# Weight sums of a one-level block product, two of four made by adding DMAs: a hybrid decoder layer on one Trainium2 core

## Chip, cores and metric

One NeuronCore of a Trainium2 chip runs the whole program in a single launch. The metric is the device time of that launch in microseconds. The program before has a median of 1208.45 us over three runs (1207.03 to 1209.76).

## What is computed

One decoder layer over 592 tokens (16 meta tokens, 8 x 8 sample tokens, 512 prompt tokens), model width 1024, all in float32:

```python
h += 0.5 * SwiGLU_1(RMSNorm(h))          # w1, w3: 1024 x 2816, w2: 2816 x 1024
h += mixer(RMSNorm(h))                   # gated DeltaNet heads and a causal convolution
h += 0.5 * SwiGLU_2(RMSNorm(h))
y  = RMSNorm(h)

def swiglu_half(h, g, w1, w3, w2):
    u = rmsnorm(h, g)
    return h + 0.5 * ((jax.nn.silu(u @ w1) * (u @ w3)) @ w2)
```

The change touches the two SwiGLU stages alone (called stages 0 and 1 in the code; of stage 1 the 16 meta tokens are dropped, so it works on 576 columns).

## The kernel before

**Number format.** Each float32 product is three float32r products: a value is split into hi (a cast on ScalarE) and lo (the rest, a subtraction on VectorE), and TensorE adds hi*hi, hi*lo and lo*hi.

**Tiles and parts.** The 2816 hidden features are 22 feature tiles of 128. A tile has two weight units in DRAM, of 128 x 1024 values (512 KB) each: unit u holds the tile's columns of w1, unit u+1 those of w3. The tiles go in parts of 4, 4, 3, 3, 4 and 4 (`PARTS`); behind each part its share of the product with w2 is made for all 8 output tiles (`down`) and added to `h` (`down_add`, L1968). The four tiles of the first part are multiplied directly.

**Seven products.** The 18 tiles of the other five parts are multiplied by a one-level scheme with seven block products in place of eight. The pair of units is taken as a 2 x 2 block matrix: A11 and A12 are the upper and lower half of the w1 unit (rows 0:4 and 4:8 of `KT`), A21 and A22 those of the w3 unit. The tokens are cut in two halves. The scheme needs four sums of weight blocks, S3, S1, S2 and S4, and four of activation blocks, T1 to T4, which are made once per stage (`half_sum`). Each block product, a seventh, is 12 matmuls of 128 x 296 (`seventh`, L839). TensorE's order within a tile is S3, S2 (behind it the mark "m6"), A12, S1 ("m5"), A11 of the next tile ("m1") or a first piece of `down`, S4 ("c1"), A22 ("c2"); see `by_sevenths` and `seventh_order`. The marks are values of the semaphore `seventh_done`.

**Where the weights lie.** `raw` and `raw2` take the two units of a tile as they come from DRAM, by turns. A set of seven pieces of 128 x 512 holds the blocks in hi and lo: `s_hi` and `s_lo`, each twice, by turns as well (`piece`, the number of the turn is `use`). The float32 sums (`s_sum`) lie in the same bytes as `s_lo`, which overwrites them.

**Who makes the sums.** VectorE makes all four, 128 x 512 each, from raw:

```python
V.tensor_tensor(s_f32(t, S3), r[:, 0, 0:4], r[:, 1, 0:4], ALU.subtract)      # sums_first, L1984
V.tensor_tensor(s_f32(t, S1), r[:, 1, 0:4], r[:, 1, 4:8], ALU.add)           # sums_first, L1985
V.tensor_tensor(s_f32(t, S2), s_f32(t, S1), raw_tile(t.u)[:, 0, 0:4], ALU.subtract)   # sum_two, L1989
V.tensor_tensor(s_f32(t, S4), raw_tile(t.u)[:, 0, 4:8], s_f32(t, S2), ALU.subtract)   # sum_four, L1993
```

While TensorE works on a tile, VectorE and ScalarE prepare the next one (`nxt` in `by_sevenths`). On ScalarE the order is: cast of A11/A12 (`hi_first`, L1393), cast of g, two copies out of PSUM behind m6 (L1478, L1480), cast of S3/S1 (`hi_sums(nxt, 0)`, L1398), copy behind m5 (L1485), cast of S2/S4 (`hi_sums(nxt, 1)`, L1398), `seed` (L1472), cast of A22 (L1402), SiLU (L1432). On VectorE: `c21` (L2018) and the gate product (L1928) of the tile before, the first two sums, rest of A11/A12 (L1997), rest of g (L1937), S2 (L1989), rest of S3/S1 (L2005), S4 (L1993), `c22` (L2024), rest of S2/S4 (L2005), rest of A22 (L2010). TensorE does not start A22 of a tile until `c22` of that tile is done. Both orders are written out by hand; each engine works its own queue strictly in order.

**Loads.** SyncE issues all weight loads in one order (`load_used`, L654): both units of a tile, once the last rest of the tile two turns back has been taken (`w_lo_ready`). GpSimd does nothing in these stages; its first work is the sum of squares behind stage 0.

## Time and profile before

| | |
|---|---|
| median of 3 runs | 1208.45 us (1207.03 to 1209.76) |
| the profiled execution | 1213.22 us, its span 1211.1 us |
| TensorE busy | 1194.6 us, 99% of the span, 8832 matmuls |
| VectorE busy | 787.3 us, 65%, 1155 instructions |
| ScalarE busy | 515.8 us, 43% |
| GpSimd busy | 75.2 us, 6% |
| DMA | 99.68 MB, mean 82 GB/s |
| mean granted TensorE clock | 0.991 |

The span runs from the first to the last instruction of one profiled execution. Busy times of the engines overlap. Matmuls are pipelined, so the duration of one is longer than the distance from one to the next.

### The profile page before, as it was taken

How to read it: one execution, taken by the hardware profiler on the slowest of the kernel's cores; microseconds unless marked ns; L12 is line 12 of the kernel's file. 1: busy time of each engine (PE TensorE's matmuls, PEld its weight loads, DVE VectorE, ACT ScalarE, POOL GpSimd, SP SyncE). 2: the span in 40 equal slices, each digit the busy share in tenths (PEclk: the TensorE clock that was granted, in tenths of full speed). 3: DMA queues.
4: the chain of work that ended last, by engine and by line, in shares of the span. 5: the costliest groups of instructions: out<-in, count | busy, mean ns of one | idle time of the engine just before them, and what ended most of it. 6: DMA issues, size and time to landing. Idle time of an engine off the chain costs nothing.

```text
span 1211.1 us, 21067 instructions
## 1 busy us (share of the span) xinstructions
PE 1194.6 (99%) x8832; PEld 1167.1 (96%) x8832; DVE 787.3 (65%) x1155; ACT 515.8 (43%) x820; POOL 75.2 (6%) x58
## 2 busy tenths in 40 slices
PE   9999999999999999999999998999999999999997
PEld 9999999999999998999989897999999999999997
DVE  6897565767566644666447786537785667675764
ACT  6345343535344542333443444433444344353355
POOL 0000000000000300000125210220000000000003
PEclk9999999999999999999999999999999999999999
DMA  5322212222223422111600002322123131222112
GB/s 189 127 86 73 105 61 96 88 105 79 96 79 109 127 73 79 60 53 54 125 4 1 1 2 88 117 84 88 53 105 109 72 116 62 96 104 105 70 71 78
DMA packets 39212, 99.68 MB, mean 82 GB/s; under 512 B 12112, under 2 KB 15568, under 8 KB 39120
## 3 DMA queue, kind: packets, MB, share of 16 engines
q1 hardware_dynamic: 38064, 96.00, 23.5%
q10 hardware_dynamic: 1056, 2.36, 0.5%
q8 instruction: 70, 1.15, 0.4%
q14 instruction: 22, 0.18, 0.1%
HBM read 92.91 MB, written 5.44 MB: 81 GB/s over the span
## 4 chain that ended last, share of the span: by engine, by line
PE 96%; DVE 2%; ACT 1%; issue 1%; DMA 0%; POOLq 0%; DVEq 0%; POOL 0%; SPq 0%
PE ps L839 34%; PE ps L806 21%; PE ps L755 20%; PE ps L951 12%; PE ps L1329 4%; PE ps L719 1%; PE ps L1135 1%; PE ps L1343 1%; PE ps L1241 1%; ACT x_hi L1411 1%; DVE w_lo L1906 1%; DVE h L1968 1%; PE ps L921 0%; PE ps L973 0%; DMA h<-x_t 0%
## 5 line engine op out<-in xcount | busy, mean ns | idle before, releaser
L839 PE MATMUL ps<-x_hi,s_hi 128*128 128x296 f32 (+1 forms) x576 | 171.2, 297 | 0.2
L839 PE MATMUL ps<-x_hi,s_lo 128*128 128x296 f32 (+1 forms) x576 | 170.9, 297 | 0.0
L839 PE MATMUL ps<-x_lo,s_hi 128*128 128x296 f32 (+1 forms) x576 | 170.9, 297 | 0.0
L755 PE MATMUL ps<-x_hi,w_hi 128*128 128x296 f32 (+1 forms) x608 | 136.8, 306 | 0.3 <-DVE x_lo L1911 0.3
L755 PE MATMUL ps<-x_lo,w_hi 128*128 128x296 f32 (+1 forms) x608 | 133.0, 300 | 0.0
L755 PE MATMUL ps<-x_hi,w_lo 128*128 128x296 f32 (+1 forms) x608 | 132.5, 299 | 0.0
L839 PE MATMUL ps<-t_hi,s_hi 128*128 128x296 f32 (+1 forms) x432 | 128.3, 297 | 0.0
L839 PE MATMUL ps<-t_hi,s_lo 128*128 128x296 f32 (+1 forms) x432 | 128.1, 297 | 0.0
L839 PE MATMUL ps<-t_lo,s_hi 128*128 128x296 f32 (+1 forms) x432 | 128.0, 296 | 0.0
L2005 DVE TENSOR_TENSOR s_lo<-s_sum,s_hi 128x1024 fp32r<-128x1024 f32 x72 | 88.2, 1225 | 44.2 <-ACT s_hi L1398 41.5
L839 PEld LDWEIGHTS ps<-x_hi,s_hi 128*128 128x128 f32 x576 | 108.4, 188 | 0.6 <-issue 0.6
L839 PEld LDWEIGHTS ps<-x_hi,s_lo 128*128 128x128 f32 x576 | 108.4, 188 | 0.0
L839 PEld LDWEIGHTS ps<-x_lo,s_hi 128*128 128x128 f32 x576 | 108.3, 188 | 0.0
L755 PEld LDWEIGHTS ps<-x_hi,w_hi 128*128 128x128 f32 x608 | 99.8, 191 | 3.7 <-issue 2.8
L1378 ACT CAST w_hi<-raw 128x1024 fp32r<-128x1024 f32 x52 | 54.1, 1043 | 114.3 <-PE ps L755 83.0
L755 PEld LDWEIGHTS ps<-x_lo,w_hi 128*128 128x128 f32 x608 | 99.9, 191 | 0.0
L755 PEld LDWEIGHTS ps<-x_hi,w_lo 128*128 128x128 f32 x608 | 99.2, 190 | 0.0
L1398 ACT CAST s_hi<-s_sum 128x1024 fp32r<-128x1024 f32 x72 | 76.0, 1056 | 46.0 <-DVE s_sum L1993 42.3
L1968 DVE SCALAR_TENSOR_TENSOR h<-ps,h 128x592 f32<-128x592 f32 (+1 forms) x92 | 69.5, 761 | 23.4 <-PE ps L806 18.1
L806 PE MATMUL ps<-g_hi,w_hi 128*128 128x296 f32 (+1 forms) x384 | 83.1, 298 | 0.0
L806 PE MATMUL ps<-g_lo,w_hi 128*128 128x296 f32 (+1 forms) x384 | 82.9, 297 | 0.0
L806 PE MATMUL ps<-g_hi,w_lo 128*128 128x296 f32 (+1 forms) x384 | 82.6, 296 | 0.0
(316 smaller groups left out, 2558.8 us busy)
## 6 DMA issues: line engine op xcount, KB each, us to landing
raw<-weights SPq DMA_DIRECT2D x150, 512.0 KB, 3.4
raw<-weights SPq DMA_DIRECT2D x16, 384.0 KB, 3.5
S<-states SPq DMA_DIRECT2D x1, 2048.0 KB, 11.8
new_state<-S ACTq DMA_DIRECT2D x1, 2048.0 KB, 6.9
y_t<-h SPq DMA_DIRECT2D x4, 336.0 KB, 2.3
h<-x_t SPq DMA_DIRECT2D x4, 296.0 KB, 4.7
h<-x_t SPq DMA_DIRECT2D x2, 592.0 KB, 7.5
raw<-weights SPq DMA_DIRECT2D x4, 256.0 KB, 5.2
```

The source lines that it names most:

```text
L719: last = nc.tensor.matmul(ps[:, u, half, 0:HALF], w[:, u, k, :], x[:, k, half * HALF:(half + 1) * HALF], start=(k == 0 and n == 0), stop=( ...
L755: last = nc.tensor.matmul(ps[:, slot if out is None else out, half, 0:w_half], w[:, slot, k, :], x[:, k, a:a + w_half], start=(k == 0 and ...
L806: last = nc.tensor.matmul(ps[:, slot, half, 0:w_half], w[:, (k % 2) * n + i, :], x[:, i, token_half(half, lo)], start=(i == 0 and r == 0), ...
L839: last = nc.tensor.matmul(out, w[:, k, :], x[:, k, :], start=(start and k == 0 and r == 0), stop=(k == KT // 2 - 1 and r == 2), skip_group ...
L951: return nc.tensor.matmul(out, lhsT, rhs, start=start, stop=stop, skip_group_check=True)
L1135: last = nc.tensor.transpose(half_bank(a + q, 0, n)[:, hd, :], inverse(t)[:, 2 * q + hd, 0:n], m("ident", n))
L1241: nc.tensor.matmul(ps[:, OUT_SLOT[j], half, 0:w_half], w[:, j, k, :], x[:, k - 4, a:a + w_half], start=(k == 4 and r == 0), stop=False, sk ...
L1329: last = nc.tensor.matmul(ps[:, OUT_SLOT[j], half, 0:w_half], w[:, j, k, :], x[:, kk, a:a + w_half], start=(u >= 2 and k == 4 and r == 0), ...
L1378: nc.scalar.copy(w_hi[:, slot], raw[:, slot % 2]).then_inc(w_hi_ready, 1)
L1398: nc.scalar.copy(piece(0, t.use, at, 2), piece(2, t.use, at, 2)).then_inc(piece_s_hi, 1)
L1968: V.scalar_tensor_tensor(two(h[:, k, lo:]), both(slot, lo), 0.5, two(h[:, k, lo:]), ALU.mult, ALU.add).then_inc(psum_free, part.step(k))
L2005: V.tensor_tensor(piece(1, t.use, at, 2), piece(2, t.use, at, 2), piece(0, t.use, at, 2).bitcast(F32), ALU.subtract).then_inc(piece_s_lo, 1)
```

## The change

1. S3 and S1 are no longer made by VectorE. SyncE loads the upper half of the w3 unit (A21, 256 KB) into both places in `s_sum` (`load_bases`), and GpSimd issues two DMAs from DRAM that add to what lies there: A11 to the place of S3, A22 to that of S1 (`add_bases`, `accum_op=ALU.add`). The upper half of the w3 unit is no longer loaded into `raw`.
2. Since these DMAs add, the second block row (the w3 unit) is taken with the other sign: S2 and S4 become additions, T1, T2 and T4 change sign (two of the activation sums become a `scalar_tensor_tensor`), and the result is taken from `h` with -0.5 in place of +0.5.
3. The waits follow. A base load of a tile waits until the block product that used this place two turns back is done ("m6" for S3, "m5" for S1, `sum_free`), and for the base load before it. An adding DMA waits for its base load and for the adding DMA before it. ScalarE's cast of S3/S1 and VectorE's S2 wait for both adding DMAs of the tile (`base_sums`).
4. The first two units of w2 in a set move from the pieces A11, A12, S3, S1 to A11, A12, S2, S4 (`down_unit`), so that the places of S3 and S1 are free during `down`.
5. Some semaphores are merged (`tables_in`, `wba_ready`).

```diff
+def summed(what, t):
+    return 2 * t + ("S2", "S4").index(what) + 1
...
             if (part.use + part.n + v // 2 + 1) % 2:
-                return [x[1][:, KT * (v % 2):KT * (v % 2 + 1)] for x in (s_hi, s_lo)]
+                at = KT // 2 * (S2 if v % 2 else A11)
+                return [x[1][:, at:at + KT] for x in (s_hi, s_lo)]
...
+        def sum_free(eng, t, at):
+
+            back = t.use - 2
+            while back >= 0:
+                for before in FFN[t.part.stage][1:]:
+                    if before.use <= back < before.use + before.n:
+                        eng.wait_ge(seventh_done, SEVENTH["m6" if at == S3 else "m5", before.tiles[back - before.use].t])
+                        return
+                back -= 2
+            eng.wait_ge(unit_done, FFN[t.part.stage][0].count(3) if back == -1 else t.part.base)
...
+            def load_tile(t):
+
+                part, use = t.part, t.use
+                if use > 1:
+                    sp.wait_ge(w_lo_ready, t.u - 2)
+                elif use == 1:
+                    sp.wait_ge(t_vector, t_dve("lo T4", part.stage))
+                for j in range(2):
+                    if use == 0:
+                        sp.wait_ge(w_lo_ready, t.u + j - 1)
+                    to, sem_in = (raw2, raw2_in) if use % 2 else (raw, raw_in[j])
+                    rows = slice(KT // 2 if j else 0, KT)
+                    sp.dma_start(to[:, j, rows], weights[t.u + j][:, rows]).then_inc(sem_in, 16)
+
+            def load_bases(t):
+
+                for i, at in enumerate((S3, S1)):
+                    sum_free(sp, t, at)
+                    if t.t or i:
+                        sp.wait_ge(base_in, 32 * t.t + 16 * i)
+                    sp.dma_start(piece(2, t.use, at), weights[t.u + 1][:, 0:KT // 2]).then_inc(base_in, 16)
+
             def load_parts(stage):
 
                 for part in FFN[stage][1:]:
                     for t in part.tiles:
-                        load_used(part, t.u, t.use, KT)
+                        for load in (load_bases, load_tile) if t.use == 1 else (load_tile, load_bases):
+                            load(t)
...
             def hi_sums(t, which):
-                act.wait_ge(weight_sums, 3 * t.t + (3 if which else 1))
+                if which:
+                    act.wait_ge(weight_sums, summed("S4", t.t))
+                else:
+                    act.wait_ge(base_sums, 32 * (t.t + 1))
...
-                V.scalar_tensor_tensor(two(h[:, k, lo:]), both(slot, lo), 0.5, two(h[:, k, lo:]), ALU.mult,
+                V.scalar_tensor_tensor(two(h[:, k, lo:]), both(slot, lo), -0.5 if part.at else 0.5, two(h[:, k, lo:]), ALU.mult,
                                        ALU.add).then_inc(psum_free, part.step(k))
...
-            def sums_first(t):
-
-                r = raw_tile(t.u)
-                raw_ready(t.u)
-                raw_ready(t.u + 1)
-                set_free(dve, t.part, t.use)
-                V.tensor_tensor(s_f32(t, S3), r[:, 0, 0:4], r[:, 1, 0:4], ALU.subtract)
-                V.tensor_tensor(s_f32(t, S1), r[:, 1, 0:4], r[:, 1, 4:8], ALU.add).then_inc(weight_sums, 1)
...
+            def sum_two(t):
+                dve.wait_ge(base_sums, 32 * (t.t + 1))
+                V.tensor_tensor(s_f32(t, S2), s_f32(t, S1), raw_tile(t.u)[:, 0, 0:4], ALU.add).then_inc(weight_sums, 1)
+
+            def sum_four(t):
+                dve.wait_ge(weight_sums, summed("S2", t.t))
+                V.tensor_tensor(s_f32(t, S4), raw_tile(t.u)[:, 0, 4:8], s_f32(t, S2), ALU.add).then_inc(weight_sums, 1)
...
-                out, a, b = {"T3": (t_sum[3][:, :, 0:n], x22, x12), "T1": (x12, x12, x11), "T2": (x22, x22, x12),
-                             "T4": (t4_f32(lo), x21, x22)}[q]
-                V.tensor_tensor(out, a, b, ALU.subtract).then_inc(t_vector, 1)
+                out, a, b = {"T3": (t_sum[3][:, :, 0:n], x22, x12), "T1": (x12, x11, x12), "T2": (x22, x12, x22),
+                             "T4": (t4_f32(lo), x22, x21)}[q]
+                if q in ("T2", "T4"):
+                    V.scalar_tensor_tensor(out, a, -1.0, b, ALU.mult, ALU.subtract).then_inc(t_vector, 1)
+                else:
+                    V.tensor_tensor(out, a, b, ALU.subtract).then_inc(t_vector, 1)
...
+            def add_bases(stage):
+
+                for part in FFN[stage][1:]:
+                    for t in part.tiles:
+                        for i, (at, j, k) in enumerate(((S3, 0, 0), (S1, 1, KT // 2))):
+                            pool.wait_ge(base_in, 32 * t.t + 16 * (i + 1))
+                            if t.t or i:
+                                pool.wait_ge(base_sums, 32 * t.t + 16 * i)
+                            pool.dma_start(piece(2, t.use, at), weights[t.u + j][:, k:k + KT // 2],
+                                           accum_op=ALU.add).then_inc(base_sums, 16)
+
+            add_bases(0)
             sum_squares(1)
...
             sum_squares(2, LATE)
+            add_bases(1)
             sum_squares(3, LATE)
```

How the instructions stand, on VectorE, in the second part of stage 0, from the end of the preparation of its second tile to that of its third. Before:

```order
L2018 TENSOR_TENSOR work<-ps,work 128x296
L1928 TENSOR_TENSOR work<-work 128x592
L1984 TENSOR_TENSOR s_sum<-raw 128x512
L1985 TENSOR_TENSOR s_sum<-raw 128x512
L1997 TENSOR_TENSOR s_lo<-raw,s_hi 128x1024
L1937 TENSOR_TENSOR g_lo<-work,g_hi 128x592
L1989 TENSOR_TENSOR s_sum<-s_sum,raw 128x512
L2005 TENSOR_TENSOR s_lo<-s_sum,s_hi 128x1024
L1993 TENSOR_TENSOR s_sum<-raw,s_sum 128x512
L2024 TENSOR_TENSOR work<-ps,work 128x296
```

With the change, the same place:

```order
L2053 TENSOR_TENSOR work<-ps,work 128x296
L1970 TENSOR_TENSOR work<-work 128x592
L2032 TENSOR_TENSOR s_lo<-raw,s_hi 128x1024
L1979 TENSOR_TENSOR g_lo<-work,g_hi 128x592
L2022 TENSOR_TENSOR s_sum<-s_sum,raw 128x512
L2040 TENSOR_TENSOR s_lo<-s_sum,s_hi 128x1024
L2026 TENSOR_TENSOR s_sum<-raw,s_sum 128x512
L2059 TENSOR_TENSOR work<-ps,work 128x296
```

The two first sums are gone; from S2 (now L2022) to `c22` (now L2059) the same four instructions stand in the same order.

On SyncE's queue, from the first tile of that part to the loads of its w2 units, with the change (before, there stand 18 rows of L654, 128x1024, one behind the other up to the end of that part and the first tiles of the next; `s_sum` are the base loads):

```order
L684 DMA raw<-weights 128x1024
L684 DMA raw<-weights 128x512
L692 DMA s_sum<-weights 128x512 x4
L684 DMA raw<-weights 128x1024
L684 DMA raw<-weights 128x512
L684 DMA raw<-weights 128x1024
L684 DMA raw<-weights 128x512
L692 DMA s_sum<-weights 128x512 x2
L684 DMA raw<-weights 128x1024
L684 DMA raw<-weights 128x512
L692 DMA s_sum<-weights 128x512 x2
L670 DMA raw<-weights 128x1024 x4
```

Each tile has two base loads behind its own loads; only the second tile has them ahead of these. The load of a fourth tile now stands behind the base loads of the third.

## Rows read from the trace of the kernel before

**Rows 1.** The page: busy time of each engine, and the granted clock in 40 slices.

```profile
PE 1194.6 (99%) x8832; PEld 1167.1 (96%) x8832; DVE 787.3 (65%) x1155; ACT 515.8 (43%) x820; POOL 75.2 (6%) x58
...
PEclk9999999999999999999999999999999999999999
```

**Rows 2.** What TensorE waited for: us in total, times, longest (8 rows in all).

```profile
PE ps L951 <- DVE qo L2446: 2.5, 2, 2.0
PE ps L1095 <- DVE d_kg L2387: 2.2, 1, 2.2
...
PE ps L951 <- ACT d_inv L1745: 0.2, 1, 0.2
```

**Rows 3.** Busy time by stretch: PE, PEld, DVE, ACT, POOL; clock, DMA share, GB/s.

```profile
20.00:60.00 40.00, 40.00 (x296) 40.00 (x295) 32.66 (x39) 16.67 (x22) 0.00 (x0) 1.00 0.37 123
...
100.00:140.00 40.00, 40.00 (x296) 40.00 (x295) 26.58 (x35) 19.76 (x30) 0.00 (x0) 1.00 0.27 100
...
470.00:500.00 30.00, 30.00 (x176) 26.41 (x175) 16.16 (x35) 11.58 (x24) 0.00 (x0) 0.89 0.17 53
```

**Rows 4.** Groups of VectorE's instructions by line: busy us, mean ns; idle before.

```profile
L2005 DVE TENSOR_TENSOR s_lo<-s_sum,s_hi 128x1024 fp32r<-128x1024 f32 x72 | 88.2, 1225 | 44.2 <-ACT s_hi L1398 41.5
...
L1984 DVE TENSOR_TENSOR s_sum<-raw 128x512 f32<-128x512 f32 x36 | 24.7, 686 | 18.7 <-PE ps L806 17.3 <-DMA raw<-weights 1.4
L1985 DVE TENSOR_TENSOR s_sum<-raw 128x512 f32<-128x512 f32 x36 | 24.6, 684 | 0.0
```

**Rows 5.** Timeline of ScalarE, marks m6 and m5 of two tiles: start us, us.

```profile
91.48 0.39 ACT L1478 COPY ps<-ps 128x296 f32<-128x296 f32 x1 [1.94 <-PE ps L839]
...
94.74 0.41 ACT L1485 COPY work<-ps 128x296 f32<-128x296 f32 x1 [1.60 <-PE ps L839]
...
102.89 0.39 ACT L1478 COPY ps<-ps 128x296 f32<-128x296 f32 x1 [1.19 <-PE ps L839]
...
103.49 1.06 ACT L1398 CAST s_hi<-s_sum 128x1024 fp32r<-128x1024 f32 x1
```

**Rows 6.** Timeline of VectorE, third tile of the second part prepared.

```profile
100.20 0.78 DVE L1928 TENSOR_TENSOR work<-work 128x592 f32<-128x592 f32 x1
...
103.92 0.68 DVE L1989 TENSOR_TENSOR s_sum<-s_sum,raw 128x512 f32<-128x512 f32 x1
104.71 1.22 DVE L2005 TENSOR_TENSOR s_lo<-s_sum,s_hi 128x1024 fp32r<-128x1024 f32 x1
105.85 0.68 DVE L1993 TENSOR_TENSOR s_sum<-raw,s_sum 128x512 f32<-128x512 f32 x1
106.59 0.47 DVE L2024 TENSOR_TENSOR work<-ps,work 128x296 f32<-128x296 f32 x1
```

**Rows 7.** TensorE: timeline, first matmul of A22 of the second tile; first product with S3.

```profile
109.21 0.30 PE L839 MATMUL ps<-x_hi,s_hi 128*128 128x296 f32 x1
...
L839 PE MATMUL ps<-t_hi,s_hi x432: 290/297/303, 88.0 to 1172.5; 128*128 128x296 f32 x72, 128*128 128x288 f32 x72
```

**Rows 8.** The loads of L654, and DMA issues by size: KB each, median us to landing.

```profile
L654 SPq DMA_DIRECT2D raw<-weights x112: 327/333/1425, 56.8 to 1165.8; - x112
...
DMA to landing us min/median/max: 2.9/3.9/6.5
y_t<-h SPq DMA_DIRECT2D x4, 240.0 KB, 2.3
```

**Rows 9.** Starts of the stage: VectorE and SyncE's timeline, then GpSimd's first work.

```profile
61.44 1.23 DVE L1906 TENSOR_TENSOR w_lo<-raw,w_hi 128x1024 fp32r<-128x1024 f32 x1 [0.29 <-ACT w_hi L1378]
...
78.11 0.68 DVE L1989 TENSOR_TENSOR s_sum<-s_sum,raw 128x512 f32<-128x512 f32 x1
...
98.11 0.80 SPq L654 DMA_DIRECT2D raw<-weights  x2
...
394.72 0.76 POOL L2593 COPY ssum<-sq 128x592 f32<-128x592 f32 x1 [394.27 <-ACT sq L1412]
```

More of the change, by code:

```diff
@@ L514, in build @@
         psum_free = sem("psum_free")
-        x_in = [sem(f"x_in{q}") for q in range(len(X_PIECES))]; vec_in = sem("vec_in"); norm_in = sem("norm_in"); hist_in = sem("hist_in"); state_in = sem("state_in")
+        x_in = [sem(f"x_in{q}") for q in range(len(X_PIECES))]; vec_in = sem("vec_in"); norm_in = sem("norm_in"); hist_in = sem("hist_in")
         ones_set = sem("ones_set")
@@ L522, in build @@
         raw2_in = sem("raw2_in")
-        weight_sums = sem("weight_sums"); piece_s_hi = sem("piece_s_hi"); piece_s_lo = sem("piece_s_lo")
+        base_in = sem("base_in"); base_sums = sem("base_sums"); weight_sums = sem("weight_sums"); piece_s_hi = sem("piece_s_hi"); piece_s_lo = sem("piece_s_lo")
         seventh_done = sem("seventh_done"); copies_out = sem("copies_out"); halves_out = sem("halves_out")
@@ L526, in build @@
         g_hi_ready = sem("g_hi_ready"); g_ready = sem("g_ready")
-        wba_hi_ready = sem("wba_hi_ready"); wba_ready = sem("wba_ready")
+        wba_ready = sem("wba_ready")
         pads_set = sem("pads_set")
@@ L532, in build @@
         sig_ready = sem("sig_ready"); c_in_ready = sem("c_in_ready")
-        dft_in = sem("dft_in"); taps_ps = sem("taps_ps"); taps_ready = sem("taps_ready")
+        tables_in = sem("tables_in"); taps_ps = sem("taps_ps"); taps_ready = sem("taps_ready")
         win_ps = sem("win_ps"); win_ready = sem("win_ready"); spec_ps = sem("spec_ps"); spec_ready = sem("spec_ready")
@@ L681, in _ @@
             sp.wait_ge(unit_done, U_GLU)
-            sp.dma_start(dft[:], dfts).then_inc(dft_in, 16)
+            sp.dma_start(dft[:], dfts).then_inc(tables_in, 16)
             with sp.Fori(0, (U_QKV + 4 - U_GLU - 4) // 2) as i:
@@ L689, in _ @@
             sp.wait_ge(unit_done, U_GLU)
-            sp.dma_start(S[:, :, 1:NG, :], states).then_inc(state_in, 16)
+            sp.dma_start(S[:, :, 1:NG, :], states).then_inc(tables_in, 16)
             sp.wait_ge(c_in_ready, NC_)
@@ L914, in gate_products @@
             def gate_products():
-                pe.wait_ge(wba_ready, 1)
+                pe.wait_ge(wba_ready, 2)
                 pe.wait_ge(rstd_ready, 2)
@@ L955, in tap_transforms @@
             def tap_transforms():
-                pe.wait_ge(dft_in, 16)
+                pe.wait_ge(tables_in, 16)
                 pe.wait_ge(psum_free, U_QKV)
@@ L1252, in state_heads @@
                 if hd == 0:
-                    pe.wait_ge(state_in, 16)
+                    pe.wait_ge(tables_in, 32)
                     pe.wait_ge(s["ek_ready"], 1)
@@ L1574, in _ @@
             nc.scalar.activation(expa[:], v("a_log", 0, H), ACT.Exp)
-            nc.scalar.copy(wba[:, :, 0:2 * H], v("w_ba", 0, KT * 2 * H).rearrange("p (k c) -> p k c", k=KT)).then_inc(wba_hi_ready, 1)
+            nc.scalar.copy(wba[:, :, 0:2 * H], v("w_ba", 0, KT * 2 * H).rearrange("p (k c) -> p k c", k=KT)).then_inc(wba_ready, 1)
             root(0)
@@ L1976, in s_f32, with lo_first @@
                 return piece(2, t.use, at)
[L1978 to L1980 removed]
+            def sum_two(t):
[4 more added lines that the diff above has]
+                V.tensor_tensor(s_f32(t, S4), raw_tile(t.u)[:, 0, 4:8], s_f32(t, S2), ALU.add).then_inc(weight_sums, 1)
+            def lo_first(t):
                 raw_ready(t.u)
[L1982 removed]
                 set_free(dve, t.part, t.use)
[L1984 to L1995 removed]
                 dve.wait_ge(piece_s_hi, 3 * t.t + 1)
@@ L2003, in lo_sums @@
                 if not which:
-                    dve.wait_ge(weight_sums, 3 * t.t + 2)
+                    dve.wait_ge(weight_sums, summed("S2", t.t))
                 V.tensor_tensor(piece(1, t.use, at, 2), piece(2, t.use, at, 2), piece(0, t.use, at, 2).bitcast(F32),
@@ L2034, in by_sevenths @@
                 if nxt:
-                    sums_first(nxt)
                     lo_first(nxt)
@@ L2091, in down_first @@
                 half_lo("B21", stage)
-                sums_first(t)
                 down_add(part, 1)
@@ L2113, in down_mid @@
                     down_add(part, k)
-                sums_first(t)
                 down_add(part, 3)
@@ L2188, in _ @@
                 add_square(k)
-            dve.wait_ge(wba_hi_ready, 1)
+            dve.wait_ge(wba_ready, 1)
             V.tensor_tensor(wba[:, :, 2 * H:], v("w_ba", 0, KT * 2 * H).rearrange("p (k c) -> p k c", k=KT),
@@ L2561, in tail_add @@
                 out = ps[:, k - TAIL_K, q, 0:TAIL[q]]
-                V.scalar_tensor_tensor(h[:, k, cols], out, 0.5, h[:, k, cols], ALU.mult, ALU.add).then_inc(psum_free, 1)
+                V.scalar_tensor_tensor(h[:, k, cols], out, -0.5, h[:, k, cols], ALU.mult, ALU.add).then_inc(psum_free, 1)
             def tail_y(j, q):
```

7 lines of the change are left out of this document (removed).

## The prediction

> **What bounds the kernel now.** I read the page's busy times first: TensorE is busy 1194.6 of 1211.1 us, VectorE 65%, GpSimd 6% [rows 1]. Then the list of what TensorE waited for: eight rows with 10.0 us in all, the longest in total 2.5 us [rows 2]. For the two stretches of the SwiGLU stages in which blocks are multiplied by sevenths (60 to 395 us and 850 to 1180 us) the same list is empty. So TensorE never waits for a weight sum today. Then the busy time by stretch: between 20 and 60 us, with VectorE busy 32.66 of 40 us, TensorE issues 296 matmuls; between 100 and 140 us, with VectorE busy only 26.58 us, again 296 [rows 3]. One matmul per 40/296 = 0.135 us, whatever VectorE does. A seventh is 12 of them, 1.63 us, and a tile seven sevenths, 11.4 us, which the two m6 marks at 91.48 and 102.89 us confirm [rows 5].
>
> **What is removed.** 36 tiles lose two sums of 0.686 and 0.684 us on VectorE, 49.3 us of 787.3 [rows 4]. Cover: all of it lies beside TensorE's work, and no wait of TensorE ends on these sums [rows 2]. Worth 0 us. The sign changes cost nothing either: four activation sums become another form of instruction with as many columns, in a place where TensorE has no wait, and -0.5 replaces 0.5. The w2 units only change their place. In `raw` 256 KB per tile are no longer loaded.
>
> **What is added.** Per tile two base loads on SyncE and two adding DMAs on GpSimd. SyncE's issues took 0.33 us each [rows 8] and go out in time it spends waiting for buffers. GpSimd is idle until 394.72 us [rows 9]; the 36 adding DMAs of stage 0 are over when the last of its tiles is prepared, a `down` of 8 x 24 matmuls, 26 us, before that; in stage 1 they follow its sum of squares. These costs are 0 on the path. What can cost something is the new wait: ScalarE's cast of S3/S1 and VectorE's S2 wait for both adding DMAs, and everything queued behind them (copy behind m5, S4, `c22`) waits too.
>
> **How late may the sums be?** Take the third tile of the second part. Its base load of S3 may start at m6 of the first tile, which ScalarE saw at 91.48 us, that of S1 at m5, 94.74 us [rows 5]. The cast of S3/S1 stood at 103.49 us [rows 5]. From there the chain is cast, rest of S3/S1 at 104.71, S4 at 105.85, `c22` at 106.59 to 107.06 us [rows 6]. TensorE needs `c22` before its first matmul of A22 at 109.21 us [rows 7], so the chain has 2.15 us to spare and the sums may land as late as 103.49 + 2.15 = 105.64 us: 14.2 us behind m6, 10.9 us behind m5. The copy behind m5 has a little more (TensorE wants it one seventh before A22, at 109.21 - 1.63 = 107.58 us, and it can be over at 104.6 + delay + 0.4).
>
> Let L be the time of a base load and A that of an adding DMA, issue to landing. The adding DMAs go one behind the other, so the conditions are L + 2A up to 14.2 us and L + A up to 10.9 us; for the fourth tile, whose DMAs queue behind those of the third, L + 4A up to 14.2 + 11.4 = 25.6 us. The first two tiles of a part have the whole `down` of 26 us (20 us with three tiles) for theirs. At the start of the stage the units are free at 61.44 + 1.23 = 62.7 us [rows 9]; with two issues of 0.4 us ahead, L + 2A may last from 63.5 to 78.11 us, where VectorE takes S2 [rows 9], that is 14.6 us, and more, since the first product with S3 comes at 88.0 us [rows 7]. The wait for m5 stands ahead of the fourth tile's own loads on SyncE; they went out at 98.11 us [rows 9], 3.4 us behind m5, so nothing is held up.
>
> **L and A.** L: 240 KB of another transfer took 2.3 us, 512 KB loads 2.9 us at the least and 3.9 us in the median [rows 8]. I take 2.9 us for 256 KB. No row shows an adding DMA or one from GpSimd. Bounds: not below the 2.3 us of a plain transfer of this size; above, the longest load of 512 KB in this stage, 6.5 us [rows 8]. I take the median of the 512 KB loads, 3.9 us, because an adding DMA of 256 KB reads 512 KB as well, half of it from SBUF. Then L + 2A = 10.7 us against 14.2, and L + 4A = 18.5 against 25.6: nobody waits for longer than the spare time. The sum is 0 us: 1211.1 us of span, 1213.2 us in the profiled run, and against the median, which lies 4.8 us below the profiled run, 1208.5 us.
>
> The Trainium skill (DMA: Bandwidth & Descriptors, Anatomy of one DMA) prices a DMA issued by GpSimd at about 2.0 us plus its bytes over 436 GB/s, which would be 2.6 us here and L + 2A = 8.1 us, so the sum would be 0 as well; no row here has such a DMA.
>
> With both at their upper ends (L = 3.9, A = 6.5) L + 2A = 16.9 us, 2.7 us too late in the third tile, and L + 4A = 29.9, 4.3 us too late by the fourth. A stage has three parts of four tiles and two of three behind the first part: 3 x 4.3 + 2 x 2.7 = 18.3 us, both stages 36.6 us. That is the far bound: 1245 us. The threshold is sharp: with L = 2.9, A = 5.65 us.
>
> **Rivals.**
>
> *The chain of DMAs becomes the bound (slower).* GpSimd's two adding DMAs, issued one behind the landing of the other, take longer than 5.7 us each; then the third and fourth tiles of each part start late. For it: transfers share the queues, the DMA load rises (768 KB more per tile, to some 127 MB from 99.7), and single loads already took 6.5 us. Against: the DMA engines are busy a quarter of the time (0.27 between 100 and 140 us [rows 3]). Price at A = 6.0: 0.7 and 1.3 us, 2 x (3 x 1.3 + 2 x 0.7) = 10.6 us, 1219 us; at the far bound 1245 us. Chance 0.21.
>
> *VectorE holds up GpSimd's issues (slower).* VectorE runs without a gap from 100.20 us to the end of `c22` at 107.06 us [rows 6], 5.6 us without the two sums. If an issue had to wait for a gap in it, 2.8 us in the mean, A is 6.7 us: 2.9 + 13.4 = 16.3, 2.1 us late, 2.9 + 26.8 = 29.7, 4.1 us late, in all 2 x (3 x 4.1 + 2 x 2.1) = 33 us, 1241 us. Against: VectorE's instructions here run at one value per cycle and partition or slower ((1225 - 684) ns for 512 more columns, 1.06 ns each [rows 4]), none in a doubled mode. Chance 0.04. The Trainium skill (SBUF — State Buffer, Who interferes with whom) says that a VectorE copy or tensor-scalar in a two-port mode locks GpSimd out of the ports it writes descriptors through, while a tensor-tensor takes only the read side; by that rule the instructions in these rows, all tensor-tensor, hold nothing up. That is why this rival stays small.
>
> *Faster.* VectorE's 49 us come back only if something waited for it. The one place I can name is the clock: it was granted at 0.89 in the mixer's 470 to 500 us and at 1.00 in the stages that change [rows 3]. A mean clock higher by 0.4% would give 4.8 us, 1203.7 us. Nothing in the change touches those stretches. Chance 0.07.
>
> *The change does not do what it says*, in that S2 and the cast merely wait where the sums stood: then VectorE's busy time falls and its idle time before S2 rises by as much, and the time stays as forecast; it is contained in it.
>
> **How the numbers follow.** 0.2% is 2.4 us, about what a measurement of this kernel tells from no change. No difference: 0.68, faster 0.07, slower 0.21 + 0.04 = 0.25. The predicted time is that of the likeliest case, 1208.5 us. Below, the range goes to 1206, the lowest run shown less 1 us. Above, it takes in the chain of DMAs up to about two thirds of the way from its threshold to its far bound, 1230 us; some 0.1 lies above, 0.05 below, and the rest of 0.2 is what I do not trust in my bounds.
>
> **What would show it.** Right: TensorE's waits still have no row of `by_sevenths`; VectorE is busy some 738 us; adding DMAs land within 3 to 5 us; ScalarE's cast of S3/S1 stands where it stood relative to m6, 0.6 us behind it. Wrong: a row TensorE waits for VectorE's `c22` or the copy behind m5, with 16 to 32 times, and adding DMAs of 5.7 us or more; or matmuls at another distance than 0.135 us in the same stretches.

## The result, and the profile after

| | before | with the change |
|---|---|---|
| median | 1208.8 us (9 runs, 1206.81 to 1209.76) | 1213.1 us (9 runs, 1211.11 to 1215.83) |
| ratio, 95% interval | | 1.0035 (1.0023 to 1.0046) |
| profiled execution, span | 1213.22 us, 1211.1 us | 1214.03 us, 1212.2 us |
| mean granted clock | 0.991 | 0.994 |

The change costs 4.3 us, 0.35%. That is inside the range of 1206 to 1230 us, but not where the prediction put most of its chance: "no difference" had 0.68, "slower" 0.25. By the prediction's own 0.2% the result is "slower", and the range holds it only because it made room for that rival.

The page of the changed kernel, busy times, the loaded bytes, the shares of the chain that ended last, and the group and the issues of the adding DMAs:

```profile
PE 1193.3 (98%) x8832; PEld 1166.4 (96%) x8832; DVE 746.2 (62%) x1083; ACT 514.0 (42%) x820; POOL 137.4 (11%) x130
...
DMA packets 59951, 128.03 MB, mean 106 GB/s; under 512 B 14416, under 2 KB 17872, under 8 KB 59856
...
PE 87%; DMA 6%; DVE 3%; ACT 2%; issue 2%; SPq 0%; POOLq 0%; DVEq 0%; POOL 0%
...
L2641 POOL DMA_DIRECT2D s_sum<-weights x72 | 62.3, 865 | 648.0 <-DMA s_sum<-weights 638.6
...
s_sum<-weights SPq DMA_DIRECT2D x72, 256.0 KB, 3.0
s_sum<-weights POOLq DMA_DIRECT2D x72, 256.0 KB, 4.5
raw<-weights SPq DMA_DIRECT2D x40, 256.0 KB, 4.5
```

VectorE has 41.1 us less to do than in [rows 1], GpSimd 62 us more, and DMA has gone from 99.68 to 128.03 MB. The work has moved as meant. The new thing stands in the third line: 6% of the chain that ends last is now a DMA, where the chain of before had 0%. By the last three lines a base load lands after 3.0 us in the median, an adding DMA of the same 256 KB after 4.5 us. A size alone does not give a time, though: the plain loads of 256 KB into `raw`, most of them issued just behind one of 512 KB, took 4.5 us as well.

What TensorE waits for, in us, times and longest. Beside the rows of the other stages, which are those of [rows 2] but for tenths, three are new, all of them in the sevenths (L878 is now the line of a seventh's matmul):

```profile
PE ps L878 <- ACT work L1527: 1.2, 3, 0.7
PE ps L878 <- DVE h L2010: 0.6, 2, 0.4
PE ps L878 <- DVE work L2059: 0.5, 3, 0.2
```

L1527 is the copy behind m5, L2059 is `c22`, L2010 the add of `down` to `h`. The copy and `c22` were named beforehand as the ones that would be late, but with 16 to 32 waits; they have six here, eight with the adds to `h`, and all eight are in stage 1. The list leaves out the shortest waits, of 0.1 us or so; the timeline shows one of these in stage 0, below. VectorE and ScalarE wait far longer than TensorE does, for the adding DMAs themselves:

```profile
DVE s_sum L2022 <- DMA s_sum<-weights: 38.0, 18, 4.1
```

```profile
ACT s_hi L1440 <- DMA s_sum<-weights: 33.2, 23, 3.4
```

38.0 us of S2 waiting and 33.2 us of the cast of S3/S1 waiting leave 2.3 us of TensorE waiting, because in most tiles what these engines do next is not yet wanted. This is why the sums of the waits say little about the price, and the place of each late one has to be looked at.

**The tile that the prediction was worked out on.** Third tile of the second part, GpSimd (start, duration, operation, idle time ahead and its cause), then ScalarE and VectorE:

```profile
94.58 0.86 POOL L2641 DMA_DIRECT2D s_sum<-weights  x1 [11.82 <-DMA s_sum<-weights]
99.88 0.86 POOL L2641 DMA_DIRECT2D s_sum<-weights  x1 [4.44 <-DMA s_sum<-weights]
```

```profile
91.67 0.39 ACT L1520 COPY ps<-ps 128x296 f32<-128x296 f32 x1 [1.94 <-PE ps L878]
...
103.09 0.39 ACT L1520 COPY ps<-ps 128x296 f32<-128x296 f32 x1 [1.18 <-PE ps L878]
...
105.30 1.05 ACT L1440 CAST s_hi<-s_sum 128x1024 fp32r<-128x1024 f32 x1 [1.50 <-DMA s_sum<-weights]
```

The first row of ScalarE is m6 of the first tile, where the base load of S3 may go. It landed by 94.58 us (L = 2.9 us), the first adding DMA by 99.88, the second by 105.30 us. The first of them landed 4.8 us after its issue, and the second went out 0.5 us later, so the first costs the chain 5.3 us; the second landed after 5.4 us. So L + 2A is 13.6 us, where I had 10.7 us against a limit of 14.2. The cast of S3/S1, 0.6 us behind m6 before [rows 5], is now 2.2 us behind it: 1.6 of the 2.15 us to spare are gone, and here TensorE still waits for nobody.

**The last tile of stage 1**, where it does. A tile of 288 columns takes 11.16 us there (m6 at 1147.37 and 1158.53), so there is less time than in stage 0. SyncE, GpSimd, ScalarE, TensorE:

```profile
1147.37 3.52 SPq L692 DMA_DIRECT2D s_sum<-weights  x2
1154.71 0.81 SPq L670 DMA_DIRECT2D raw<-weights  x2
```

```profile
1150.38 0.86 POOL L2641 DMA_DIRECT2D s_sum<-weights  x1 [5.00 <-DMA s_sum<-weights]
1155.66 0.86 POOL L2641 DMA_DIRECT2D s_sum<-weights  x1 [4.42 <-DMA s_sum<-weights]
```

```profile
1158.53 0.38 ACT L1520 COPY ps<-ps 128x288 f32<-128x288 f32 x1 [1.15 <-PE ps L878]
...
1162.59 1.05 ACT L1440 CAST s_hi<-s_sum 128x1024 fp32r<-128x1024 f32 x1 [3.36 <-DMA s_sum<-weights]
1163.54 0.39 ACT L1527 COPY work<-ps 128x288 f32<-128x288 f32 x1
```

```profile
1162.84 0.29 PE L878 MATMUL ps<-x_lo,s_hi 128*128 128x288 f32 x1
1162.97 0.29 PE L878 MATMUL ps<-x_hi,s_lo 128*128 128x288 f32 x1
1163.98 0.40 PE L878 MATMUL ps<-x_hi,s_hi 128*128 128x288 f32 x1 [0.72 <-ACT work L1527]
1164.22 0.29 PE L878 MATMUL ps<-x_lo,s_hi 128*128 128x288 f32 x1
1164.35 0.29 PE L878 MATMUL ps<-x_hi,s_lo 128*128 128x288 f32 x1
```

Base load 3.0 us, first adding DMA 5.3 to the next issue, second, with the two raw loads of 1154.71 just ahead of it, 6.9: the sums land 15.2 us behind m6 of 1147.37. The cast waited, and the copy behind m5, which stands behind it on ScalarE though its own product was long finished, waited with it. Then TensorE lost 1163.98 - 1162.97 - 0.13 = 0.88 us at the stall and 0.11 us more at the next matmul. The list of waits shows 0.72 of this 0.99 us, because it counts from the end of the matmul before, and that one's row lasts 0.29 us where the starts are 0.13 us apart. Without the 0.88 us the copy would have been in time, so its limit is 15.22 - 0.88 = 14.3 us. `c22`, which stands behind S2 and S4 on VectorE, then stalled TensorE once more, by 0.33 us at 1166.01 us. Its limit in this stage is thus 15.22 - 0.88 - 0.11 - 0.33 = 13.9 us, and the two other fourth tiles of the stage give the same.

By the same reading (cast of S3/S1 less m6 two tiles back) the sums of the six fourth tiles came 14.57, 14.35 and 13.47 us behind it in stage 0, and 14.77, 14.67 and 15.22 us in stage 1, each of these three with stalls; those of the ten third tiles 12.5 to 14.1 us, without one. The second adding DMA of a fourth tile, issue to landing, took 5.1 to 6.9 us, that of a third tile 4.3 to 5.6 us. SyncE issues two raw loads shortly ahead of each of these, the first of them 0.2 to 1.4 us ahead in fourth tiles and 1.5 to 2.2 us ahead in third ones; no run moves these loads alone, so that they are the cause is not shown.

The 14.57 us of stage 0 did not pass quite unseen. `c22` and TensorE there:

```profile
120.48 0.46 DVE L2059 TENSOR_TENSOR work<-ps,work 128x296 f32<-128x296 f32 x1
```

```profile
120.68 0.30 PE L878 MATMUL ps<-x_hi,s_lo 128*128 128x296 f32 x1
121.09 0.37 PE L878 MATMUL ps<-x_hi,s_hi 128*128 128x296 f32 x1
```

The two matmuls start 0.41 us apart in place of 0.135: the second came 0.28 us late, behind the end of `c22` at 120.94 us. That puts the limit of `c22` in stage 0 at 14.57 - 0.28 = 14.3 us.

**The start of a part behind one of three tiles** was not foreseen. VectorE, stage 1:

```profile
1000.36 0.69 DVE L2022 TENSOR_TENSOR s_sum<-s_sum,raw 128x512 f32<-128x512 f32 x1 [0.46 <-DMA s_sum<-weights]
...
1006.19 0.75 DVE L2010 SCALAR_TENSOR_TENSOR h<-ps,h 128x576 f32<-128x576 f32 x1
```

S2 of the part's first tile waits for the adding DMAs, and the adds of `down` to `h`, which free TensorE's result banks, are queued behind S2. The first matmul of the part's first A11 then waited for one of them:

```profile
1007.09 0.37 PE L878 MATMUL ps<-x_hi,s_hi 128*128 128x288 f32 x1 [0.20 <-DVE h L2010]
```

**Where the 4.3 us are in the trace.** The same stretch, from the last matmul on x_hi and w_lo of the directly multiplied first part of stage 1 to GpSimd's first row on the sum of squares behind it, lasts 325.5 us before and 329.2 us after; stage 0 ends at 394.72 us [rows 9] and at 395.32 us:

```profile
395.32 0.76 POOL L2628 COPY ssum<-sq 128x592 f32<-128x592 f32 x1 [30.61 <-ACT sq L1454]
...
1186.88 0.68 POOL L2628 COPY ssum<-sq 128x576 f32<-128x576 f32 x1 [30.36 <-ACT sq L1454]
```

That is 3.7 us in stage 1. Stage 0, measured in the same way from its own first part, lasts 334.75 us before and 335.15 us after, 0.4 us more, and this is the short stall at 121.09 us with a still smaller one at 301 us; the four kernels below without a stall in that stage have 334.7 to 334.8 us. Summed over the eight stalls, the matmuls' starts lie 4.3 us further apart than at their regular distance. The kernel before has two stalls of 0.3 us each itself in stage 1, for adds to `h` at 1008.51 and 1061.40 us, so that 3.7 us are left; with the 0.4 us of stage 0 the trace accounts for 4.1 of the 4.3 us. The two profiled spans differ by only 1.1 us because the mixer between the stages, which the change does not touch, took 465.5 us in one and 462.4 us in the other. TensorE's clock was granted differently there; the row of 470 to 500 us (columns as in [rows 3], where it reads 0.89) with those of the changed stretches:

```profile
100.00:140.00 40.00, 39.88 (x293) 39.67 (x292) 24.28 (x31) 19.67 (x30) 4.20 (x5) 1.00 0.49 141
470.00:500.00 30.00, 30.00 (x188) 27.07 (x187) 17.07 (x36) 11.57 (x24) 0.00 (x0) 0.94 0.16 54
```

So stage durations are compared below, not spans.

### The profile page after: what moved, and what is told of

It is laid out like the page before. It is cut to its first block, busy times and chain, and to the rows that moved or that the text cites. A ratio compares the mean times of both kernels' runs of the same rounds, so it can differ in the third digit from the quotient of the medians.

```text
span 1212.2 us, 21281 instructions
## 1 busy us (share of the span) xinstructions
PE 1193.3 (98%) x8832; PEld 1166.4 (96%) x8832; DVE 746.2 (62%) x1083; ACT 514.0 (42%) x820; POOL 137.4 (11%) x130
## 2 busy tenths in 40 slices
DMA packets 59951, 128.03 MB, mean 106 GB/s; under 512 B 14416, under 2 KB 17872, under 8 KB 59856
## 4 chain that ended last, share of the span: by engine, by line
PE 87%; DMA 6%; DVE 3%; ACT 2%; issue 2%; SPq 0%; POOLq 0%; DVEq 0%; POOL 0%
PE ps L878 28%; PE ps L794 20%; PE ps L845 18%; PE ps L990 12%; DMA s_sum<-weights 6%; PE ps L1368 4%; PE ps L758 1%; PE ps L1174 1%; DVE h L2010 1%; PE ps L1382 1%; PE ps L1280 1%; ACT x_hi L1453 1%; DVE w_lo L1948 1%; PE ps L949 0%; ACT s_hi L1440 0%
## 5 line engine op out<-in xcount | busy, mean ns | idle before, releaser
L878 PE MATMUL ps<-x_hi,s_hi 128*128 128x296 f32 (+1 forms) x576 | 171.8, 298 | 2.5 <-ACT work L1527 1.2
L878 PE MATMUL ps<-x_lo,s_hi 128*128 128x296 f32 (+1 forms) x576 | 170.9, 297 | 0.0
L878 PE MATMUL ps<-x_hi,s_lo 128*128 128x296 f32 (+1 forms) x576 | 170.8, 297 | 0.0
L2641 POOL DMA_DIRECT2D s_sum<-weights x72 | 62.3, 865 | 648.0 <-DMA s_sum<-weights 638.6
L878 PE MATMUL ps<-t_hi,s_hi 128*128 128x296 f32 (+1 forms) x432 | 128.3, 297 | 0.0
L878 PE MATMUL ps<-t_hi,s_lo 128*128 128x296 f32 (+1 forms) x432 | 128.1, 297 | 0.0
L878 PE MATMUL ps<-t_lo,s_hi 128*128 128x296 f32 (+1 forms) x432 | 128.0, 296 | 0.0
L878 PEld LDWEIGHTS ps<-x_hi,s_hi 128*128 128x128 f32 x576 | 108.3, 188 | 4.5 <-issue 2.5
L878 PEld LDWEIGHTS ps<-x_hi,s_lo 128*128 128x128 f32 x576 | 108.4, 188 | 0.0
L878 PEld LDWEIGHTS ps<-x_lo,s_hi 128*128 128x128 f32 x576 | 108.3, 188 | 0.0
L2010 DVE SCALAR_TENSOR_TENSOR h<-ps,h 128x592 f32<-128x592 f32 (+1 forms) x92 | 69.7, 763 | 44.2 <-PE ps L845 43.5
```

The lines of the kernel that those rows point to most:

```text
L878: last = nc.tensor.matmul(out, w[:, k, :], x[:, k, :], start=(start and k == 0 and r == 0), stop=(k == KT // 2 - 1 and r == 2), skip_group ...
L2010: V.scalar_tensor_tensor(two(h[:, k, lo:]), both(slot, lo), -0.5 if part.at else 0.5, two(h[:, k, lo:]), ALU.mult, ALU.add).then_inc(psum_ ...
L2641: pool.dma_start(piece(2, t.use, at), weights[t.u + j][:, k:k + KT // 2], accum_op=ALU.add).then_inc(base_sums, 16)
```

## Experiments

**First question: what of the change costs anything?** Theory: the serial chain of base load and two adding DMAs. Rivals: the signs, the added DMA traffic, GpSimd's issues beside VectorE.

**Adding DMAs of a tile in flight together.** The second no longer waits for the first (they add to different places):

```diff
-                            if t.t or i:
-                                pool.wait_ge(base_sums, 32 * t.t + 16 * i)
+                            if t.t and not i:
+                                pool.wait_ge(base_sums, 32 * t.t)
```

> The second adding DMA of a tile no longer waits until the first has landed; both may be in flight. Theory A (the chain of base load and two adding DMAs, 2.9 + 2 x 5.3 us = 13.6 us behind m6, is at its limit of 14.2 us, and less in the second stage): the chain falls to m5 + 2.9 + 5.3 us, some 11.5 us behind m6, TensorE's waits for ScalarE's copy behind m5, for c22 and for the add to h go, and the time returns to that of the kernel before, 1208 to 1210 us. Theory B (the added DMA traffic or the other edits slow the stages): no change, 1212 to 1214 us.

Measured: 1209.57 us, ratio to before 0.9996 (0.9985 to 1.0006); stage 1 325.2 us, and the list of TensorE's waits has no row of the sevenths. The work, the bytes and the engines are those of the change; only the moment of the second adding DMA differs. So neither the traffic nor GpSimd's issues cost anything by themselves. In the last tile the cast that started 4.06 us behind m6 (1162.59 against 1158.53) now starts 1.58 us behind it (m6 at 1157.45):

```profile
1159.03 1.05 ACT L1440 CAST s_hi<-s_sum 128x1024 fp32r<-128x1024 f32 x1 [0.88 <-DMA s_sum<-weights]
```

The loss is there only when the two adding DMAs go one behind the other. The expected 11.5 us was not met, though. The sums of the six fourth tiles come 11.7 to 12.7 us behind m6 two tiles back, 1.5 to 3.0 us sooner than in the change. Those of the third tiles come no sooner on the whole, 12.1 to 14.2 us. One of them, in stage 1 with m6 two tiles back at 1064.82 us:

```profile
1078.97 1.05 ACT L1440 CAST s_hi<-s_sum 128x1024 fp32r<-128x1024 f32 x1 [2.29 <-DMA s_sum<-weights]
```

That is 14.15 us against the 13.9 us of `c22` in that stage, and TensorE is 0.25 us late at 1082.40 us, too little for the list of waits. The second adding DMA of a third tile now takes 5.4 to 8.0 us to landing, where it took 4.3 to 5.6 us with the first one out of the way. What is gained is in the fourth tiles, and there it is enough.

**Signs alone**, all sums on VectorE as before:

```diff
-                V.tensor_tensor(s_f32(t, S3), r[:, 0, 0:4], r[:, 1, 0:4], ALU.subtract)
+                V.tensor_tensor(s_f32(t, S3), r[:, 0, 0:4], r[:, 1, 0:4], ALU.add)
...
-                V.tensor_tensor(out, a, b, ALU.subtract).then_inc(t_vector, 1)
+                if q in ("T2", "T4"):
+                    V.scalar_tensor_tensor(out, a, -1.0, b, ALU.mult, ALU.subtract).then_inc(t_vector, 1)
+                else:
+                    V.tensor_tensor(out, a, b, ALU.subtract).then_inc(t_vector, 1)
```

> The kernel before with the signs of the change alone: all four weight sums on VectorE as additions, T1, T2, T4 with the other sign, -0.5 for +0.5; no new DMA. Theory A: the time of the kernel before within 0.1%. Theory C (the sign change costs something, two activation sums in another form of instruction): part of the 4.3 us, 1210 us or more.

Measured: 1209.08 us, 0.9997 (0.9982 to 1.0011), stage 1 325.5 us as before. No cost of the signs can be seen.

**One adding DMA per tile**: S3 by DMA, S1 by VectorE, the w3 unit loaded whole.

```diff
-                    rows = slice(KT // 2 if j else 0, KT)
+                    rows = slice(0, KT)
...
-                for i, at in enumerate((S3, S1)):
+                for i, at in enumerate((S3,)):
...
+            def sum_one(t):
...
+                V.tensor_tensor(s_f32(t, S1), r[:, 1, 0:4], r[:, 1, 4:8], ALU.add).then_inc(weight_sums, 1)
```

> S3 alone is made by an adding DMA, S1 by VectorE from raw (the w3 unit is loaded whole again, 1024 KB + 512 KB per tile moved, as much data from DRAM as with two sums less 256 KB). Theory A: the chain is 2.9 + 5.3 = 8.2 us behind m6, no wait of TensorE in the stages, time of the kernel before, 1208 to 1210 us. Theory B (traffic): 1211 to 1213 us.

Measured: 1209.0 us, 0.9999 (0.9983 to 1.0014), no wait of TensorE in the sevenths. An adding DMA that has no other one ahead of it costs nothing here, though its bytes are loaded all the same. It is also faster. The 36 of this kernel landed in 3.6 to 3.9 us:

```profile
s_sum<-weights POOLq DMA_DIRECT2D x36, 256.0 KB, 3.7
```

The 72 of the change, with two base loads per tile and a second adding DMA around them, took 3.7 to 7.2 us, 4.5 in the median. Which of the neighbours slows them was not tried.

**Each adding DMA in two halves**, one behind the other, to measure A at another size and to see the chain well over its limit:

```diff
-                            if t.t or i:
-                                pool.wait_ge(base_sums, 32 * t.t + 16 * i)
...
+                            for n in range(2):
+                                if t.t or i or n:
+                                    pool.wait_ge(base_sums, 64 * t.t + 32 * i + 16 * n)
+                                pool.dma_start(piece(2, t.use, at)[:, 2 * n:2 * n + 2], weights[t.u + j][:, k + 2 * n:k + 2 * n + 2],
+                                               accum_op=ALU.add).then_inc(base_sums, 16)
```

> Each adding DMA is cut into two of 128 KB, one behind the landing of the other. Theory A with a cost that is mostly fixed (about 4.9 us from issue to issue each): the sums land 2.9 + 4 x 4.9 = 22.5 us behind m6, 8 us too late in the third tile, 16 us by the fourth, and GpSimd's chain of 19.6 us per tile exceeds the 11.4 us of TensorE: 1300 to 1370 us. If an adding DMA costs in proportion to its bytes (2.7 us for 128 KB), the chain stays as long as it is, 1213 us.

Measured, in two runs only: 1320.21 us, 1.0909 (1.088 to 1.0938). GpSimd and TensorE's waits:

```profile
94.77 0.86 POOL L2642 DMA_DIRECT2D s_sum<-weights  x1 [5.29 <-DMA s_sum<-weights]
98.64 0.86 POOL L2642 DMA_DIRECT2D s_sum<-weights  x1 [3.00 <-DMA s_sum<-weights]
102.07 0.86 POOL L2642 DMA_DIRECT2D s_sum<-weights  x1 [2.57 <-DMA s_sum<-weights]
105.73 0.86 POOL L2642 DMA_DIRECT2D s_sum<-weights  x1 [2.79 <-DMA s_sum<-weights]
```

```profile
PE ps L878 <- ACT work L1527: 50.7, 21, 5.0
PE ps L878 <- DVE h L2010: 22.9, 6, 6.2
```

The three distances are 3.87, 3.43 and 3.66 us, in the mean 3.65 us for 128 KB, against 5.3 us for 256 KB. That gives an estimate of a part that does not depend on the size, 2 x 3.65 - 5.3 = 2.0 us from issue to issue, and 1.65 us per 128 KB (some 79 GB/s). It comes from one tile of each kernel and includes the 0.5 us between a landing and the next issue. The waits of TensorE are the same two rows as in the change, grown: first the copy behind m5, then the adds to `h`. They make 73.6 of the 110.5 us that it is slower than the 1209.68 us of before in this set. The rest is about what TensorE's clock costs. The two stages, busy time by stretch as in [rows 3]:

```profile
60.73:446.36 385.63, 351.22 (x2454) 346.90 (x2454) 205.81 (x255) 141.85 (x210) 62.43 (x73) 0.96 0.43 115
905.60:1293.68 388.08, 345.55 (x2453) 341.15 (x2452) 203.84 (x253) 141.27 (x211) 62.26 (x72) 0.94 0.42 109
```

Before, the granted clock is 1.00 in both stages. Here, where TensorE stops for up to 6.2 us at a time, it falls to its lower level, 1.2 GHz, again and again: 4% of 385.6 us and 6% of 388.1 us, an estimate of 39 us.

**The change once more**, beside the experiments of the second question:

> The change itself once more, on the chip of the three kernels below, so that they are compared with it too. Expected: 1212 to 1214 us, ratio about 1.0035; TensorE's waits in the seven-product stages in the fourth tiles of the parts of stage 1 (copy behind m5, c22) and at the start of one or two parts (add to h), 4 us with the slow restart behind each.

Measured: 1213.84 us, 4.0 us above the 1209.86 us of before in this set, 1.0043 (1.0026 to 1.006), stage 1 328.0 us, five waits of TensorE on the same three lines, 1.4 us in all. The loss is there again, on another chip than that of the first four experiments.

**Second question: which tiles lose the time?** Base loads ahead of the tile's own loads at the start of every part (today SyncE holds them behind `raw` loads that wait for the rests of w2):

```diff
-                        for load in (load_bases, load_tile) if t.use == 1 else (load_tile, load_bases):
+                        for load in (load_bases, load_tile) if t.use == 1 or (t.i == 0 and t.use) else (load_tile, load_bases):
```

> The change with one order turned: the two base loads of the first tile of every part go ahead of that tile's own loads (as they do already for the second tile of the stage), so its sums are ready some us earlier; the adding DMAs stay one behind the other. If the waits for the add to h at a part's start (two waits, 1.1 us in the profile) came from S2 waiting with the adds queued behind it, these two go and the waits in the fourth tiles stay: 1211 to 1213 us. If the start of the parts were the main cause, the time would return to 1209 us.

Measured: 1211.15 us, 1.0014 (1.0002 to 1.0026). SyncE at the part of 1000 us, change and experiment:

```profile
983.90 0.80 SPq L684 DMA_DIRECT2D raw<-weights  x2
984.80 4.56 SPq L692 DMA_DIRECT2D s_sum<-weights  x2
```

```profile
978.78 4.39 SPq L692 DMA_DIRECT2D s_sum<-weights  x2
984.12 10.12 SPq L684 DMA_DIRECT2D raw<-weights  x4
```

The bases go out 6.0 us sooner, S2 starts at 1000.02 us without a wait, and no row of TensorE waits for L2010 any more. Two waits for L1527 (1.1 us) and four for L2059 (0.7 us) remain, all in fourth tiles but for one of 0.2 us in the last tile of a part of three, and with them a loss. The execution in the trace, at 1213.90 us the slowest of the eleven, lost almost as much as the change in its stages: 335.9 us in stage 0 and 328.4 us in stage 1. So the trace shows which waits are gone, and only the median that time is won.

**The other half alone**: in flight together only in third and fourth tiles.

```diff
-                            if t.t or i:
+                            if (t.t and not i) or (i and t.i < 2):
```

> The two adding DMAs of a tile are in flight together for the third and fourth tiles of a part alone; for the first and second they stay one behind the other. The waits in the fourth tiles should go and those for the add to h at the start of a part stay. If the fourth tiles made most of the 4 to 5 us, 1209.5 to 1211 us; if the starts of the parts made most of it, 1212 to 1213 us. With the run that put the base loads first (1.0014 over the kernel before) this gives both shares.

Measured: 1211.33 us, 1.0014 (1.0002 to 1.0026), stage 0 335.15 us, stage 1 326.2 us; two waits of TensorE in the sevenths, 0.2 us each, none for L1527. One is for an add to `h` at the start of a part of stage 0; the other is for `c22` in the last tile of stage 1, a fourth tile, where the expectation had none.

**Both repairs together:**

> Both repairs: adding DMAs of a tile in flight together and base loads of a part's first tile first. No wait of TensorE in the stages is left to remove (the first repair alone left none), so the time stays that of the kernel before, 1208 to 1210 us, and is not better: VectorE's 41 us less buy nothing. A time below 1207 us would say that something besides waits of TensorE is gained.

Measured: 1209.54 us, 1.0005 (0.9994 to 1.0016), stage 1 324.9 us, no wait. It does not beat the kernel before, it equals it. Each repair alone takes the loss from 0.35-0.43% to 0.14%, and the intervals are too wide to say by these which share is the larger. The change's own trace speaks for the fourth tiles: the two stalls at starts of parts make 1.1 us of its 4.7 us of stalls, and the kernel before loses 0.7 us at the same two places.

**Third question: does the law hold between 13.6 us and the halves?** Only the second adding DMA is halved, three in a row: L + 5.3 + 2 x 3.65 = 15.5 us.

```diff
+                            for n in range(1 + i):
+                                r0, r1 = (2 * n, 2 * n + 2) if i else (0, 4)
...
+                                if t.t or i:
+                                    pool.wait_ge(base_sums, 48 * t.t + 16 * (i + n))
...
```

> Of the two adding DMAs of a tile the second alone is cut in two halves; all three go one behind the other. By the measured steps (5.35 us for 256 KB, 3.7 us for 128 KB) the chain is 2.9 + 5.35 + 7.4 = 15.65 us behind m6, 1.45 us too late in the third tile, and 2.9 + 2 x 12.75 = 28.4 us by the fourth, 2.8 us too late; in stage 1, whose tile is 0.3 us shorter, 1.8 and 3.5 us. Sum 3 x 2.8 + 2 x 1.45 + 3 x 3.5 + 2 x 1.8 = 25.4 us over the kernel before: 1234 us, between 1228 and 1242. If the limit of the chain were not the cause, the time would rise by no more than the few us that the added traffic costs, or not at all.

Measured: 1251.89 us, 42.0 us above the median of before, 1.0372 (1.0349 to 1.0395), more than expected and outside the stated window. TensorE:

```profile
PE ps L878 <- ACT work L1527: 15.0, 15, 1.8
PE ps L878 <- DVE h L2010: 11.7, 5, 2.9
PE ps L878 <- DVE work L2059: 1.3, 8, 0.2
```

The excess is not in the third and fourth tiles but, as I read it, in the second row, five waits of up to 2.9 us for adds to `h`, at starts of parts. The test of that reading is the same kernel with the bases first:

> Three adding DMAs per tile one behind the other (1251.9 us, where 1234 us was expected) with the base loads of a part's first tile ahead of its own loads. If the 18 us that the expectation missed came from the start of the parts (TensorE waited 11.7 us for adds to h, which are queued behind S2 of the next part's first tile), these waits go and 1230 to 1240 us are left. If they came from the third and fourth tiles, the time stays near 1252 us.

Measured: 1237.23 us, 27.5 us above the 1209.70 us of before in its set, 1.0226 (1.0204 to 1.0247), in the expected window:

```profile
PE ps L878 <- ACT work L1527: 14.1, 12, 1.9
PE ps L878 <- DVE h L2010: 1.5, 3, 0.9
```

The row of L2010 fell from 11.7 to 1.5 us, and the loss by 14.5 us; the row of L1527 stayed. The 27.5 us that are left are near the 25.4 us worked out for third and fourth tiles.

## Why the prediction was right or wrong

- **TensorE waits for no weight sum before; VectorE's 49 us are worth 0.** Right. The kernel with both repairs has all of VectorE's time freed and no wait in the list, and is as fast as before (1.0005). One number was off: I expected 738 us of VectorE and it is 746.2. The durations of [rows 4] overlap with their neighbours', and busy time counts an overlap once: 41.1 us for 72 instructions is 0.57 us each, not 0.685.
- **Signs, w2 units, SyncE's issues, bytes: 0.** Right for the signs (own run). The rest is contained in the two kernels that have it and equal the kernel before; it was not tried piece by piece. The bytes cost nothing by themselves, but the loads beside them may be what makes A longer.
- **The limit of 14.2 us behind m6.** Right for stage 0, for which it was worked out: `c22` has 14.3 us there, and the copy has more, as said. In stage 1, whose tiles are 0.26 us shorter, `c22` has 13.9 us and the copy 14.3 us. That the stages differ, and that nearly all stalls would be in the second, I had not worked out.
- **L + 4A for the fourth tile.** Not the condition that decides here. It holds once two adding DMAs take longer than a tile, 2A over 11.4 us. At the A of this kernel the third tile's are over (105.30 us) before the fourth's first may go (106.20 us), so the condition of the fourth is L + 2A as well, from its own m6.
- **A = 3.9 us, "because an adding DMA of 256 KB reads 512 KB as well".** This is the step that failed. In its place the runs show 5.3 us per adding DMA in the chain of the worked tile, and 6.9 us for the second one of the last tile. The 3.9 us fits an adding DMA in the kernel with one per tile, 3.7 us; the reason given for the number was not put to a test. Missing were two things: the 0.5 us from a landing to the next issue, which the sum puts at nothing, and the longer landing among the other loads and adding DMAs of the change, 4.5 us in the median and up to 7.2. The prediction's first rival named the second of these ("transfers share the queues") and got 0.21. The threshold of 5.65 us is only 0.3 us above the 5.3. With 5.3 us in the place of 3.9 the sum is 13.5 us against 14.2; with the 6.9 us that the second can take in a fourth tile it is 15.1, and a few late tiles with some us in all is what it should have said. That the time still lay in the range is owed to the room left for the rival, and not to the sum. The 1219 us for A = 6.0 counted every third and fourth tile as late, where of the third tiles none was.
- **The skill's figure.** The Trainium skill (DMA: Bandwidth & Descriptors, Anatomy of one DMA) gave 2.6 us as the estimate for such a DMA. The trace does not agree: 4.5 us to landing in the median, and 3.7 us for one by itself. By that figure the chain would be 8.1 us, and the halves, at an estimated 2.3 us each, would have cost nothing; they cost 110.5 us.
- **"The first two tiles of a part have the whole `down`".** Second step that failed. On SyncE the base loads of a part's first tile stand behind its raw loads, which wait for the rests of w2; and behind S2 on VectorE stand the adds to `h`. I had asked what is queued behind the cast and behind S2 inside a part only. It is the smaller one: 1.1 of the 4.7 us of stalls in the change's trace, and in the kernel with three adding DMAs per tile its repair took away 14.5 of 42.0 us.
- **The rival of VectorE holding up GpSimd's issues.** Rightly small: GpSimd's issues take 0.86 us in all the rows above and 1.0 us at the most over all 72, and the kernel with both in flight has as many of them and no loss. (The 5.6 us of its working is 5.5, 6.86 - 1.37, which changes nothing.) The Trainium skill's rule (SBUF — State Buffer, Who interferes with whom), by which a tensor-tensor takes only the read side of the ports that VectorE shares with GpSimd, is in agreement with them.
- **Faster by a better clock.** Not seen. The mixer's length varies between executions (459 to 465.5 us in the profiles), with and without the change, and the medians with both repairs show no gain.

## What to carry to other kernels

A DMA that takes over work of an engine takes over its place in a chain as well: add up issue, landing, the 0.5 us or so from a landing to the next issue, and every serial DMA between the moment the buffer comes free and the moment the data is wanted, for the tightest stage and for the start of each part, and compare with the slack. Take for each DMA the time that it needs among its neighbours, and not only the median: here the sum of 13.6 us was under the limit of 14.2 us, and the tiles in which one DMA took 6 to 7 us made the loss. When the sum is that near to the limit, forecast a small loss, not none. And when two transfers do not depend on each other, let them fly together before anything else is tuned: here the loss was gone with that one wait.

## What was not expected of the hardware

- An adding DMA of 256 KB from DRAM into SBUF landed in 3.7 us (3.6 to 3.9) where there was one per tile, and in 4.5 us (3.7 to 7.2) where there were two one behind the other. Base loads of the same size took 3.0 us in the change. By the halves it costs an estimated 2.0 us plus 1.65 us per 128 KB, issue to issue.
- In flight together, two of them take 4.3 us to landing in the median, but up to 8.0 us: the second one gained nothing in the third tiles and enough in the fourth.
- A short wait of TensorE costs more than the list of waits shows: eight waits of 2.3 us in all moved the matmuls behind them by 4.3 us. At 1163.98 us it was 0.99 us for 0.72 us listed.
- A TensorE that is stopped often loses clock too: with stops of up to 6.2 us the granted clock was 0.96 and 0.94 in stages where it is 1.00 without them.
